# Moving the token tiles and the weight slots of a two-block kernel to other byte offsets in SBUF

## The reference

```python
def pool_mixer_layer(x, norm_g, w_in, w_group, scale, w_out):
    h = rmsnorm(x, norm_g)
    proj = h @ w_in                                      # 2048 x 8192
    ...
    y = jnp.einsum('bsgc,gcd->bsgd', pooled, w_group)    # 4 x 1024 x 1024
    y = y * scale * jax.nn.silu(gate)
    return x + y @ w_out                                 # 4096 x 2048
...
def conv_ffn(h, w_up, conv_w, conv_b, w_down):
    u, g = jnp.split(h @ w_up, 2, axis=-1)               # 2048 x 11264
    u = causal_conv_of_width_3(u)
    return (jax.nn.silu(u) * g) @ w_down                 # 5632 x 2048
```

## Time and profile before

| | |
|---|---|
| times of two runs | 2078.23 and 2126.14 us (median 2102.18) |
| profiled execution, its span | 2078.1 us (this is the run of 2078.23 us) |
| TensorE: matmul busy, loads busy | 2047.4 us (99%), 2017.3 us (97%), 17698 of each |
| VectorE, ScalarE, GpSimd busy | 1567.2 us (75%), 1030.4 us (50%), 15.4 us (1%) |
| DMA | 483 MB, mean 232 GB/s |
| mean granted clock of TensorE | 0.992 |

### The profile page before, as it was taken

One profiled execution on the slowest core, in us unless ns is written; L12 is line 12 of the kernel. 1 busy time (PEld: TensorE's weight loads), 2 busy tenths in 40 slices (PEclk: granted clock), 3 DMA queues, 4 the chain that ended last, 5 costly groups with the idle time before them and its releaser, 6 DMA issues.

```text
span 2078.1 us, 41240 instructions
## 1 busy us (share of the span) xinstructions
PE 2047.4 (99%) x17698; PEld 2017.3 (97%) x17698; DVE 1567.2 (75%) x2256; ACT 1030.4 (50%) x1339; POOL 15.4 (1%) x23
## 2 busy tenths in 40 slices
PE   8999999999999999998999999999999999999998
PEld 7999999999999999998999899999999999999998
DVE  7988788688687888877855687678876766666666
ACT  6444444444445466654457557454444444444444
POOL 1000000000000000000000000000000000000000
PEclk9999999999999999999999999999999999999999
DMA  8897888889685788658653754668876666666663
GB/s 272 291 355 279 290 306 304 272 281 329 217 271 160 237 286 298 218 180 311 224 165 106 195 175 131 209 205 320 307 234 194 192 196 194 191 199 194 194 193 122
DMA packets 248749, 483.01 MB, mean 232 GB/s; under 512 B 26347, under 2 KB 59735, under 8 KB 248311
## 3 DMA queue, kind: packets, MB, share of 16 engines
q1 hardware_dynamic: 247807, 480.16, 70.0%
q0 software_dynamic: 528, 0.15, 0.0%
q10 hardware_dynamic: 232, 0.06, 0.0%
HBM read 478.17 MB, written 8.44 MB: 234 GB/s over the span
## 4 chain that ended last, share of the span: by engine, by line
PE 95%; DMA 2%; DVE 2%; ACT 1%; issue 0%; POOL 0%; SPq 0%; DVEq 0%; ACTq 0%; POOLq 0%
PE acc L1930 89%; PE side L1930 3%; PE sums L1930 2%; DMA mod_raw<-in_w_mod 2%; DVE w_lo L1205 1%; PE sums L2205 1%; DVE mod_raw L1193 0%; DMA vec_rows<-in_b_q_norm_g 0%; PE sums L2013 0%; ACT w_hi L637 0%; POOL vec_rows L611 0%; DVE xT L1335 0%; POOL vec_rows L607 0%; ACT silu_row L732 0%; SPq L451 0%
## 5 line engine op out<-in xcount | busy, mean ns | idle before, releaser
L1205 DVE TENSOR_TENSOR w_lo<-raw,w_hi 128x1024 fp32r<-128x1024 f32 x681 | 830.6, 1229 | 403.2 <-ACT w_hi L637 396.3
L637 ACT ACTIVATE w_hi<-raw 128x1024 fp32r<-128x1024 f32 x681 | 718.7, 1060 | 818.9 <-PE acc L1930 701.0
L1930 PE MATMUL acc<-h_hi,w_hi 128*128 128x256 f32 x3600 | 851.4, 280 | 10.9 <-DVE xT L1335 6.6
L1930 PE MATMUL acc<-h_lo,w_hi 128*128 128x256 f32 x3600 | 843.3, 278 | 0.0
L1930 PEld LDWEIGHTS acc<-h_hi,w_hi 128*128 128x128 f32 x3600 | 677.5, 189 | 21.9 <-issue 14.3
L1930 PEld LDWEIGHTS acc<-h_lo,w_hi 128*128 128x128 f32 x3600 | 677.3, 189 | 0.1
L1930 PE MATMUL acc<-h_hi,w_lo 128*128 128x256 f32 x3600 | 486.8, 278 | 0.3 <-DVE w_lo L1205 0.3
L1930 PEld LDWEIGHTS acc<-h_hi,w_lo 128*128 128x128 f32 x3600 | 446.2, 189 | 0.4 <-DVE w_lo L1205 0.4
L1193 DVE SCALAR_TENSOR_TENSOR mod_raw<-mod_raw,silu_row 128x1024 f32<-128x1024 f32 x192 | 234.1, 1219 | 15.7 <-DMA mod_raw<-in_w_mod 15.6
L1930 PE MATMUL acc<-f_hi,w_hi 128*128 128x256 f32 x704 | 164.4, 277 | 0.0
L1930 PE MATMUL acc<-f_lo,w_hi 128*128 128x256 f32 x704 | 164.2, 276 | 0.0
(11 more groups left out here) (338 smaller groups left out, 2108.2 us busy)
## 6 DMA issues: line engine op xcount, KB each, us to landing
mod_raw<-in_w_mod SPq DMA_DIRECT2D x192, 512.0 KB, 6.4
raw<-in_w_up SPq DMA_DIRECT2D x176, 512.0 KB, 4.4
raw<-in_a_w_in SPq DMA_DIRECT2D x128, 512.0 KB, 5.2
raw<-in_w_down SPq DMA_DIRECT2D x88, 512.0 KB, 4.6
raw<-in_a_w_out SPq DMA_DIRECT2D x64, 512.0 KB, 5.4
raw<-in_w_in SPq DMA_DIRECT2D x52, 512.0 KB, 3.7
raw<-in_b_w_in SPq DMA_DIRECT2D x40, 512.0 KB, 5.2
raw<-in_a_w_group SPq DMA_DIRECT2D x32, 512.0 KB, 5.4
```

Of the source, the lines that this page charges most:

```text
L637: last = act.activation(w_hi[s][:, :], raw[s][:, :], ACT.Copy)
L1205: last = dve.tensor_tensor(w_lo[s][:, :], raw[s][:, :], f32(w_hi[s][:, :]), ALU.subtract)
L1930: return pe.matmul(o, lhsT, rhs, start=start, stop=stop, skip_group_check=True)
```

## The change

The constants move, so that `MID`, `H_AT` and `FAR` are multiples of 1024, and with them the token tiles that begin there (the tiles `y_mid_hi` and `y_mid_lo` lie 12800 bytes above `MID`, a multiple of 256 and 512). `W_AT` becomes a multiple of 256, and slot `s` of `w_hi` and `w_lo` lies `W_PAD[s]` = 0, 96, 160 or 224 bytes above one. `w_lo` begins 16384 + 256 bytes above `w_hi`. `tmp` and `mixw_hi` move up by 64 bytes, to a multiple of 256. The slots get letters for names (`w_hi_a` ...). The `raw` slots stay where they are, 128 above a multiple of 256. No instruction, wait, transfer or size changes.

```diff
-LOW, MOD_AT, W_AT, MID, H_AT, FAR = 16512, 73824, 82048, 114880, 148288, 181056
-TMP_AT = LOW + 4 * KD * TOK + 4 * RING * SLAB + 64
+LOW, MOD_AT, W_AT, MID, H_AT, FAR = 16512, 73824, 82176, 115712, 148480, 181248
+W_PAD = (0, 96, 160, 224)
+TMP_AT = LOW + 4 * KD * TOK + 4 * RING * SLAB + 128
...
-        low("tmp_gap", [P, 16])
+        low("tmp_gap", [P, 32])
...
-        ring = home(W_AT, MID)
-        w_hi = [ring(f"w_hi{s}", [P, SLAB], F32R) for s in range(RING)]
-        w_lo = [ring(f"w_lo{s}", [P, SLAB], F32R) for s in range(RING)]
+        def w_slot_at(part, s):
+
+            at = W_AT + part * (16384 + 256) + s * 4096 + W_PAD[s]
+            return home(at, MID)
+
+        w_hi = [w_slot_at(0, s)(f"w_hi_{'abcd'[s]}", [P, SLAB], F32R) for s in range(RING)]
+        w_lo = [w_slot_at(1, s)(f"w_lo_{'abcd'[s]}", [P, SLAB], F32R) for s in range(RING)]
...
-        far = home(FAR + 16384, MOD_RAW_AT - 1024)
+        far = home(FAR + 16384, MOD_RAW_AT)
```

## The result

| | before | after |
|---|---|---|
| times | 2078.23, 2126.14 us (median 2102.18) | 2145.41, 2147.83 us (median 2146.62) |
| ratio after / before | | 1.0325, 95% interval 1.0281 to 1.0370 |
| span of the profiled execution | 2078.1 us | 2143.6 us |
| TensorE matmul busy | 2047.4 us | 2115.0 us |

The changed kernel is slower. None of the 50 runs of the kernel before that this document draws on took over 2127.3 us. It is the outcome of rival 2.

The account below looks back on a forecast made before the run. TensorE bounds the kernel, by number of matmuls times spacing. From 2078.1 us, less 12 (all fast) gives 2066; plus 16,344 x 2.0 ns = 33 us gives 2099 us, range 1992 to 2157 us.

Parts of the forecast that it names:

- rival 2: Weight loads of slots b, c, d and jumps at each slab: no settling, 117.8 to 119 ns, 2140 to 2159 us; chance 0.20.
- What bounds the kernel, and by what: TensorE, busy 99% of the span: time is matmuls times spacing, two steady spacings, 113.3 and 117.8 ns, kept until disturbed.
- The second run of before: The 2126.14 us run: 47.9 us more, explained by one or both long undisturbed stretches entered in the slow spacing.
- Split engines, waits, DMA at nothing: No instruction added or removed, so 0 us for issue, waits, DMA; ScalarE and VectorE offsets 0, bounds -1 to +5 us.
- The token tiles: Token tiles, including those in `MID`, get one alignment, so what sets `y_mid` and `y` apart is gone.
- The weight slots: the step that failed: Offset jumps at each slab, stream chooses again 681 times; 115.3 ns of the attentions taken for whole kernel, plus 33 us.
- sign of being wrong in kind: In the profile after: one slot letter has a spacing none of the rows has, or TensorE begins to wait for `w_lo`.
- Rival 1: Load reads colliding with moving reads: new offsets miss the collision, 109 instead of 113.3 ns, 1996 us; chance 0.27.
- Rival 3: All slabs: each jump throws the stream out of the slow spacing but not the fast one, 2066 us; chance 0.15.
- The rule on SBUF: TensorE reading slabs: by the skill it never waits for SBUF, so the offset does nothing, time stays 2078 or 2126.

Follow-up runs that it names:

- Run 1: Changed kernel with all eight weight slots 64 bytes above a multiple of 256; 2105.2 to 2126.7 us, ratio 1.0115 to the kernel before.
- run 9: Changed kernel with all eight weight slots 88 bytes above a multiple of 256; twelve runs, median 2096.28 us, ratio 0.9973 to the kernel before.
- run 12: Changed kernel with slots a and c 64, b and d 88 bytes above a multiple of 256; median 2092.67 us, ratio 0.9987 to the kernel before.
- run 2: Changed kernel with all eight weight slots at multiples of 256 (distance 0); 2169.87 us.
- run 5: Kernel before with only its tokens moved to multiples of 1024, weight slots unmoved (distance 128); 2149.59 to 2149.74 us, ratio 1.0268.
- run 3: Changed kernel with slots a to d at 32, 64, 128 and 192 bytes above a multiple of 256; 2131.54 us.
- run 4: Changed kernel with the token tiles at MID, H_AT and FAR 64 bytes higher, weight slots unmoved; 2144.44 us.
- run 11: Changed kernel with slots a to d at distances 136, 168, 200 and 232; 2142.30 us.

## Why the prediction was wrong

*What bounds the kernel, and by what.* Right. The time is matmuls times spacing, and the spacing hangs on the distance: no instruction changed, and 65 us came. Right also, and shown in runs 1 and 9: a distance can have two steady spacings, and a stream keeps the one it is in for hundreds of microseconds.

*The second run of before.* The reading of 2126 us as two slow stretches fits. Run 1 shows a profile at 2126.7 us with exactly that. Over all experiments, the 48 further runs of the kernel before fall into groups with gaps between them: 13 from 2077 to 2082 us, 6 from 2098 to 2100, 19 from 2104 to 2109 and 10 from 2117 to 2127. From the windows, about 4,510 matmuls of the first stretch at +4.45 ns are 20 us, the 6,336 of the feed-forward (264 slabs) 28 us, both 48 us: 2098, 2106 and 2126. Five runs from 2117 to 2122 us fit none of these sums. No unprofiled run can be looked into, so this remains an argument.

*Split engines, waits, DMA at nothing.* Right: 4.4 us more VectorE time in all, 0.7 of ScalarE, and no new wait.

*The token tiles.* Right that `y_mid` and `y` would become alike; they did, at 118.6 and 118.3 ns, near the slower value.

*The weight slots: the step that failed.* The prediction said that each jump makes the stream choose again between the two spacings of the trace, and took the 115.3 ns of the attentions for the whole kernel. The runs showed instead that the 113.3 ns of distance 64 was not seen as a steady spacing at any of the four new distances. It was held over many slabs at 64 and 88 only, and now and then over a slab or a few at others (192 in the earlier trace rows). The four new distances have 119.6, 117.6, 119.7 and 116.6 ns in nearly every slab. Nor does a jump have to make the stream choose: run 12 held 113.3 ns through one at each slab. The prediction's own sign of being wrong in kind, a slot with a spacing that none of its rows has, came true with the 116.6 ns of slot d. The term was 16,344 x 2.0 ns = 33 us; with the measured mean it is 16,344 x (118.4 - 113.3) = 83 us, and 2066 + 83 = 2149 us against a measured span of 2143.6 (the sum starts from a span as well). Of the 6 us left over, 2 are time in which TensorE had no matmul: 30.7 us before, 28.6 after. The rest was not traced.

The error behind the step: the attentions are a stretch with many pauses at *one* distance. They showed how a disturbed stream divides between the spacings of distance 64. They could say nothing of the spacings that other distances have. Rows that did speak of other distances were at hand, 117.9 ns for `y_mid` and 119 ns for the slab with two alignments; I used them as bounds and gave them a fifth of the chance.

*Rival 2 (2140 to 2159 us).* Its price and its deciding point of 118.1 ns were right, its mechanism only in part. "Needs the distance of 64" is nearly so: 88 reached 113.3 ns as well. Starts that are 32 bytes off a 64-byte boundary do not sort the slots: c, at 160, and a, at 0, are the slow ones, and d, at 224, is the fastest. The jumps cost nothing that shows: distance 0 has 120.0 ns without any (run 2) and 119.6 with them, 128 has 118.7 (run 5) and 118.4 (run 3), and run 12 holds 113.3 ns with a jump at each slab.

*Rival 1 (conflict gone, 109 ns).* None of the 28 distances measured came under 113.3 ns as a steady spacing. *Rival 3 (all fast)* fell with the first window.

*The rule on SBUF.* By the Trainium skill's "SBUF — State Buffer", section "SBUF: two separate sides", TensorE never waits on anyone for SBUF. The prediction read this as "the offset does nothing", and so read it is refuted by runs 2 and 5: 120.0 and 118.7 ns against 113.3 for the same instructions on other addresses. Since only the distance between the two operands counts (run 4), it is TensorE's own two streams that disturb each other; by what mechanism no run shows. The Trainium skill says in the same section that a DMA does not slow a compute engine. The trace agrees: the spacing was 120.0 ns at DMA shares of 0.83 and 0.62 (run 2).

## What to carry to other kernels

When TensorE is busy all the time, measure its spacing, not its busy share: take a window that it filled, and divide by the count; where tiles at different addresses give different spacings for the same shape, the placement is worth up to 6% (113.3 to 120.0 ns here). What counted here is the distance between the stationary and the moving operand, and a round start was no merit: the neatest distance, 0, was the slowest. Where equal kernels give times in a few separate groups, look for two spacings in one trace before you trust a median of two runs; and a mean spacing taken at one placement says nothing of another, which has to be measured (four slots with four distances give four values in one profile).

## What the runs showed of the hardware that was not expected

Many patterns of a steady stream last a whole number of 6.67 ns, which is 16 periods of 2.4 GHz. 113.3 ns is 17 of them, and 120.0 is 18. Three matmuls at 117.8 are 53 (353.3 ns). Slot d of the changed kernel repeats after four matmuls (116, 117, 120, 113 with roundings: 466.7 ns, 70). The uniform stream at distance 128 repeats after five (115, 118, 122, 120, 119: 593.3 ns, 89). The slower stream at 88 repeats after six (115, 118, 116, 117, 116, 118: 700 ns, 105). One pattern does not fit: slot c of run 11 (distance 200) goes 116, 117, 117 all through, and 350 ns is 52.5 of them. Starts are recorded in whole ns, so a unit of half the size fits all of these, and the long patterns would fit many units. What the unit stands for was not shown, nor why 8 bytes of distance matter (80 against 88). Which of two spacings a stream takes after a pause, and how to make it take the faster one, stays open as well.
